# The entrance of the second block: order of the last GLU round, of level six and of the head factors

## What is computed

```
h  = h + conv_glu_ffn(rmsnorm(h))        # gelu(conv3(h Wa)) * (h Wb), then W_down; 11 rounds of 256 columns
z  = rms_norm(x) @ w_in                  # split into lru_x, lru_y, hg_q, hg_f, hg_i, hg_g, cq, ck, cv
ya = rglru_group(...)                    # first branch, a linear recurrence
yb = hgrn2_group(q, f, i, g, ...)        # "third branch" of the change's title: gated linear attention, 4 heads of 64
yb = rms_norm(o per head) * silu(g)
yc = moba_group(cq, ck, cv)              # causal attention, 8 heads of 64
x  = x + concat(rms_norm(ya), yb, rms_norm(yc)) @ w_out
x  = x + relu(rms_norm(x) @ w_ff1)^2 @ w_ff2
```

## Time and profile before

| what | value |
|---|---|
| median of 3 runs | 731.07 us (728.11 to 731.2) |
| profiled execution | 729.23 us, of which 727.5 us are the profile's span |
| PE, share of the span | 97% |
| DVE, ACT, POOL | 74%, 54%, 3% |
| mean granted clock of TensorE | 0.999 |
| chain that ended last | PE 74%, DVE 14%, ACT 8%, issue 3% |

### The profile page before, as it was taken

How to read it: one execution, slowest core, us unless ns; L and a number is a source line. 1 busy time by engine, 2 the same in 40 slices (tenths; PEclk the granted TensorE clock), 3 DMA queues, 4 the chain that set the end, 5 groups by cost and what they waited for, 6 DMA issues and landing times.

```text
span 727.5 us, 14613 instructions
## 1 busy us (share of the span) xinstructions
PE 705.1 (97%) x6156; PEld 665.2 (91%) x6156; DVE 537.0 (74%) x953; ACT 389.5 (54%) x599; POOL 23.9 (3%) x50
## 2 busy tenths in 40 slices
PE   7999999999999999999999999999999999999997
PEld 6998988888999999999999999888899998998995
DVE  6898898556988877777768798965977655666653
ACT  7586458356466354444445683488664334434443
POOL 3001000000000000000000240000000000000000
PEclk9999999999999999999999999999999999999999
DMA  8751253133555555555555534333345555565541
GB/s 246 219 161 59 77 158 116 62 100 134 173 173 176 174 177 194 200 184 174 177 193 197 188 130 163 122 100 125 125 147 183 202 193 175 194 209 175 182 166 58
DMA packets 94701, 115.66 MB, mean 159 GB/s; under 512 B 7972, under 2 KB 83933, under 8 KB 94637
## 3 DMA queue, kind: packets, MB, share of 16 engines
q1 hardware_dynamic: 94244, 114.51, 48.0%
q0 software_dynamic: 128, 0.13, 0.1%
q10 hardware_dynamic: 264, 0.10, 0.1%
HBM read 113.69 MB, written 1.05 MB: 158 GB/s over the span
## 4 chain that ended last, share of the span: by engine, by line
PE 74%; DVE 14%; ACT 8%; issue 3%; POOL 0%; DVEq 0%; POOLq 0%; ACTq 0%
PE psum L1838 16%; PE psum L1839 15%; PE psum L1840 15%; PE psum L2425 4%; PE psum L2423 4%; PE psum L2424 4%; DVE w_lo L1101 4%; ACT w_hi L501 3%; PE psum L2192 2%; PE psum L2190 2%; PE psum L2188 2%; DVE sz L1020 1%; PE psum L1985 1%; PE psum L2020 1%; PE psum L1930 1%
## 5 line engine op out<-in xcount | busy, mean ns | idle before, releaser
L1101 DVE TENSOR_TENSOR w_lo<-w_raw,w_hi 128x2048 fp32r<-128x2048 f32 x105 | 239.4, 2288 | 71.6 <-ACT w_hi L501 71.4
L501 ACT ACTIVATE w_hi<-w_raw 128x2048 fp32r<-128x2048 f32 x105 | 199.1, 1906 | 54.8 <-PE psum L2425 39.4
L1838 PE MATMUL psum<-x2n_hi,w_hi 128*128 128x256 f32 x400 | 114.2, 286 | 2.3 <-DVE w_lo L1101 1.2
L1839 PE MATMUL psum<-x2n_lo,w_hi 128*128 128x256 f32 x400 | 112.0, 280 | 0.0
L1840 PE MATMUL psum<-x2n_hi,w_lo 128*128 128x256 f32 x400 | 111.9, 280 | 0.0
L1838 PE MATMUL psum<-hs_hi,w_hi 128*128 128x256 f32 (+1 forms) x352 | 99.5, 283 | 0.0
L1839 PE MATMUL psum<-hs_lo,w_hi 128*128 128x256 f32 (+1 forms) x352 | 99.1, 282 | 0.0
L1840 PE MATMUL psum<-hs_hi,w_lo 128*128 128x256 f32 (+1 forms) x352 | 99.0, 281 | 0.0
L1838 PEld LDWEIGHTS psum<-x2n_hi,w_hi 128*128 128x128 f32 x400 | 75.2, 188 | 5.6 <-DVE x2n_lo L1558 1.7
L1840 PEld LDWEIGHTS psum<-x2n_hi,w_lo 128*128 128x128 f32 x400 | 76.2, 190 | 0.0
L1839 PEld LDWEIGHTS psum<-x2n_lo,w_hi 128*128 128x128 f32 x400 | 75.1, 188 | 0.6
(11 more groups left out here) (460 smaller groups left out, 1533.6 us busy)
## 6 DMA issues: line engine op xcount, KB each, us to landing
w_raw<-in_w_ff_dram SPq DMA_DIRECT2D x32, 1024.0 KB, 5.3
w_raw<-in_w_in_dram SPq DMA_DIRECT2D x27, 1024.0 KB, 5.3
w_raw<-in_w_up_dram SPq DMA_DIRECT2D x22, 1024.0 KB, 5.1
w_raw<-in_w_down_dram SPq DMA_DIRECT2D x11, 1024.0 KB, 5.0
w_raw<-in_w_o_dram SPq DMA_DIRECT2D x4, 1024.0 KB, 5.2
w_raw<-in_w_out_dram SPq DMA_DIRECT2D x4, 1024.0 KB, 5.2
w_raw<-in_w_ssm_out_dram SPq DMA_DIRECT2D x2, 1024.0 KB, 5.0
w_raw<-in_w_att_out_dram SPq DMA_DIRECT2D x2, 1024.0 KB, 4.9
```

The source lines that it names most:

```text
L501: A.activation(w_hi[:, u % NW, :], raw[:, u % NRAW, :], ACT.Copy).then_inc(sem("hi_ready"), 1)
L1101: V.tensor_tensor(w_lo[:, u % NRAW, :], raw[:, u % NRAW, :], w_hi[:, u % NW, :].bitcast(F32), ALU.subtract).then_inc(sem("lo_ready"), 1)
L1838: T.matmul(out_, lh, rh, start=start, stop=False)
L1839: T.matmul(out_, lh, rl, start=False, stop=False)
```

## The change

Five edits, all of order or of the form of a small product. In the last GLU round both engines' `split_to` for down 10 comes after the gate product: on ACT after the gelu and the copy of up_b, on DVE after `ff_lo` (in `lo_upto`). ACT's high half of hg_q comes right after that of hg_f, ahead of `x2n_hi` and the squares. DVE's low half of cq 0 comes ahead of eight tiny instructions of 2 columns (L1670 to L1677). For the second pair of heads DVE has the low half of cv 0 ahead of `m_max(1)`, and `level(5)` ahead of `m_norm(1)`; PE has `h_scores(6)` ahead of `m_turn(1)`. The head factors are made with tokens on the partitions: 128 x 8 in place of 4 x 256. In the loop of the second norm, ACT's high half of ff1 1 comes after the last two tiles.

```diff
@@ -292,7 +292,6 @@
         sq2 = sb("sq2", [P, 2, 256], F32, k(103552))
         sq3 = sb("sq3", [P, 2, 256], F32, k(107648))
         rst2 = sb("rst2", [P, 256], F32, k(105600))
-        rsm2 = sb("rsm2", [4, 256], F32, k(106624))
         sqs = sb("sqs", [P, 8, 256], F32, k(89216))
         rst1 = sb("rst1", [P, 258], F32, k(112768))
         lru_w = sb("lru_w", [P, 2, 2, P], F32, k(109696))
@@ -789,11 +788,14 @@
                     copy_up_b(i)
                 else:
                     gelu_a(i)
-                split_to(unit_at[(second, i)]["n"] + 3)
+                if i < KF // 2 - 1:
+                    split_to(unit_at[(second, i)]["n"] + 3)
                 if second == "up_b":
                     copy_up_b(i)
                 else:
                     gelu_a(i)
+                if i == KF // 2 - 1:
+                    split_to(unit_at[(second, i)]["n"] + 3)
                 if i == KF // 2 - 2:
                     act.wait_ge(sem("tiny_v"), 1)
                     A.activation(sm("sp_e", 2), sm("sp_ab", 2), ACT.Exp, scale=-1.0).then_inc(sem("tiny_a"), 1)
@@ -805,10 +807,7 @@
                     if i >= 2:
                         need(act, "acc_unit_done", i - 1)
                     A.activation(ff_hi[:, i % 2, m, :], ff[:, i % 2, m, :], ACT.Copy).then_inc(sem("ff_hi"), 1)
-            split_to(unit_at[("down", KF // 2 - 1)]["n"] + 1)
-
-
-            split_to(unit_at[("hg_f", 0)]["n"] + 1)
+            split_to(unit_at[("hg_q", 0)]["n"] + 1)
 
             def x2_square(m):
                 A.activation(sqs[:, m, :], x2[:, m, :], ACT.Square).then_inc(sem("x2_stat_sq"), 1)
@@ -821,7 +820,6 @@
                     x2_square(m // 2)
             for m in range(4, 8):
                 x2_square(m)
-            split_to(unit_at[("hg_q", 0)]["n"] + 1)
             act.wait_ge(sem("x2_stat"), 1)
             A.activation(rst1[:, :], banks[3][:, 0:258], ACT.Sqrt, bias=eps_col, scale=1.0 / D).then_inc(
                 sem("x2_rms"), 1)
@@ -944,7 +942,7 @@
                 scaled("lru_y", m, lru_g, ACT.Gelu_apprx_tanh)
 
             act.wait_ge(sem("hg_stat"), 2)
-            A.activation(rsm2[:, :], banks[5][0:4, 0:256], ACT.Sqrt, bias=eps_col[0:4, :], scale=1.0 / 64).then_inc(
+            A.activation(sm("hg_root", 8), banks[5][:, 0:8], ACT.Sqrt, bias=eps_col, scale=1.0 / 64).then_inc(
                 sem("hg_rms"), 1)
             act.wait_ge(sem("yc_stat"), 4)
             A.activation(rst3[:, :], banks[6][:, 0:256], ACT.Sqrt, bias=eps_col, scale=1.0 / 512).then_inc(
@@ -976,7 +974,7 @@
                     sem("x3_hi"), 1)
                 need(act, "x3_stat_sum", min(m - 1, max(m - 2, 1)))
                 A.activation(sq2[:, m % 2, :], x2[:, m, :], ACT.Square).then_inc(sem("x3_stat_sq"), 1)
-                if m % 2 and m < 6:
+                if m % 2 and m < 4:
                     split_to(unit_at[("w_out2", m // 2)]["n"] + 4)
             split_to(unit_at[("ff1", 0)]["n"] + 2)
             act.wait_ge(sem("norm_sum"), 2)
@@ -1666,6 +1665,7 @@
 
             for m in range(2):
                 scale("hg_f", 0, m, hgf[:, m, :])
+            two_after("hg_f")
             dve.wait_ge(sem("tiny_a"), 3)
             seq(V.tensor_scalar(sm("sp_m", 2), lam, -1.0, 0.0, ALU.mult, ALU.max))
             seq(tt(sm("sp_m", 2), sm("sp_m", 2), sm("sp_l", 2), ALU.add))
@@ -1675,7 +1675,6 @@
             seq(V.tensor_scalar(sm("lb_m", 2), sm("lb_0", 2), TINY, None, ALU.max))
             seq(V.tensor_scalar(sm("lb_c", 2), sm("lb_0", 2), -1.0, 1.0, ALU.mult, ALU.add))
             V.tensor_scalar(sm("n8sp", 2), sm("sp_m", 2), -8.0, None, ALU.mult).then_inc(sem("tiny_v"), 1)
-            two_after("hg_f")
             dve.wait_ge(sem("w2_act"), 4)
             for m in range(2):
                 seq(V.tensor_scalar(hgf[:, m, :], hgf[:, m, :], sm("lb_c", 2)[:, m:m + 1], sm("lb_m", 2)[:, m:m + 1],
@@ -1706,11 +1705,11 @@
             scale("cq", 1, 0, cq[:, 2, :], 0.125)
             level(4)
             scale("cq", 1, 1, cq[:, 3, :], 0.125)
+            two_after("cq", 1)
             m_max(1)
-            two_after("cq", 1)
             scale("ck", 1, 0, ck[:, 2, :])
+            level(5)
             m_norm(1)
-            level(5)
             two_after("ck", 1)
             scale("ck", 1, 1, ck[:, 3, :])
             level(6)
@@ -1743,7 +1742,7 @@
                 dve.wait_ge(sem("w2_act"), 7 + m)
                 tt(xc[:, m, :], lru_r[:, m, :], lru_g[:, m, :], ALU.mult).then_inc(sem("lru_h"), 1)
             dve.wait_ge(sem("hg_rms"), 1)
-            V.reciprocal(rsm2[:, :], rsm2[:, :]).then_inc(sem("hg_r"), 1)
+            V.reciprocal(sm("hg_root", 8), sm("hg_root", 8)).then_inc(sem("hg_r"), 1)
             dve.wait_ge(sem("yc_rms"), 1)
             seq(V.reciprocal(rst3[:, :], rst3[:, :]))
             scale("hg_g", 0, 0, hgg[:, 0, :])
@@ -2264,16 +2263,23 @@
                 last.then_inc(sem("hg_o"), 1)
 
             def hg_stat():
-                for m in range(2):
-                    pe.wait_ge(sem("hgo"), m + 2)
-                    T.matmul(banks[5][0:4, 0:256], sel[:, m, 0, 0:4], hqf[:, m, :], start=(m == 0),
-                             stop=(m == 1)).then_inc(sem("hg_stat"), 1)
+                for t in range(2):
+                    for m in range(2):
+                        pe.wait_ge(sem("hgo"), m + 2)
+                        last = T.matmul(banks[5][:, 4 * t:4 * t + 4], hqf[:, m, P * t:P * t + P], sel[:, m, 0, 0:4],
+                                        start=(m == 0), stop=(m == 1))
+                    last.then_inc(sem("hg_stat"), 1)
 
             def hg_bc():
                 pe.wait_ge(sem("hg_r"), 1)
                 for m in range(2):
-                    T.matmul(banks[4 + m][:, 0:256], selT[0:4, m, :], rsm2[:, :], start=True,
-                             stop=True).then_inc(sem("hg_bc"), 1)
+                    for t in range(2):
+                        for par in range(2):
+                            c = 4 * t + 2 * m + par
+                            last = T.matmul(banks[4 + m][64 * par:64 * par + 64, P * t:P * t + P],
+                                            sm("hg_root", 8)[:, c:c + 1].to_broadcast([P, 64]), ident[:], start=True,
+                                            stop=True, skip_group_check=True)
+                    last.then_inc(sem("hg_bc"), 1)
 
             def m_scores(pr):
 
@@ -2342,8 +2348,8 @@
             unit("cq", 1, x2n, 8, between=both((m_turn, 0), (h_scores, 4)))
             m_scores(1)
             unit("ck", 1, x2n, 8, between=lambda: h_scores(5))
+            h_scores(6)
             m_turn(1)
-            h_scores(6)
 
             def gates_and_level():
                 lru_gates()
```

## The result

The changed kernel took 726.65 us (median of 20 runs), the one before 730.67 us in 20 runs beside them: a ratio of 0.9945, with a 95% interval of 0.9932 to 0.9959. That is 4.0 us less, between 3.0 and 5.0. The time lies in the forecast's range, 1.25 us under the 727.9 us that it named. One of the 20 runs before took 977.54 us, which hardly moves a median.

A forecast was written before the change was run, and what follows sets the result against it. PE, busy 97% of the span, was taken to bound the kernel, with about 7 us of stops as ceiling. Gains 1.8 + 0.35 + 0.43 + 0.65 = 3.2 us off 731.07 gave 727.9 us, range 725.6 to 730.0.

The forecast's parts named there:

- part 1: Last GLU round, first norm and cq 0: h_scores(1) starts at 436.8, a gain of 1.8 us.
- The moved low half collides with POOL: Rival at cq 0: DVE pays 0.8 us beside POOL's masks, part 1 gives 1.0, total 728.7 us; chance 0.1.
- hg_q's high half: ACT's half, moved up, fits between `ff_hi` and the first x2, 407.8 to 409.7; no gain of its own.
- The rival on the slower side: ACT's hg_q half waits for its raw unit; landing after 408.4 delays the norm, up to 736.6 us; chance 0.04.
- named as a sign of being wrong: Signs listed beforehand included ACT waiting for a transfer before hg_q's half, and a PE stop ahead of ff1 1.
- Part 2: Level six, second pair of heads: cv 0 starts at 470.0 instead of 470.36, 0.35 us, bounds 0 and 0.6.
- Part 3: Head factors: shorter reciprocal on DVE, hg_g's evacuation moves from 511.38 to 510.95, a gain of 0.43 us.
- `hg_bc`: Head factors' product on PE, 4 records to 16: extra cost between nothing and 0.8 us, taken as nothing.
- Part 4: Second norm: PE's whole 0.53 us stop at ff1 0 goes, 0.65 us with its restart; bound 0.3 to 0.7.
- barely covered: ff1 1's half, next late after the second norm: DVE ends it at 545.7, PE wants it at 545.8.
- the 0.63 given to one side of it: Chance 0.63 that the measured change lies within 0.5% of the time before.
- the 0.33 given to the other: Chance 0.33 that the changed kernel is faster by over 0.5%.

The follow-up runs named there:

- e10: Changed kernel with POOL's memset of hA moved ahead of the six masks, second profile: 723.74 us, ratio to before 0.9952; end 332.88 us after up_a 10.
- e3: Changed kernel with DVE's eight tiny instructions ahead of the low half of cq 0 again: end 333.29 us after up_a 10, against 333.47.
- e7: Changed kernel with POOL's memset of hA moved ahead of the six masks, first profile: end 333.05 us after up_a 10, against 333.47.
- e5: Changed kernel with ACT's high half of ff1 1 ahead of the second norm's last two tiles again: end 334.28 us after up_a 10, against 333.47.
- e6: Changed kernel with the head factors as 4 rows of 256 tokens again: end 334.22 us after up_a 10, against 333.47.
- e1: Changed kernel with the last GLU round in its old order on ACT and DVE: end 335.10 us after up_a 10, against 333.47.
- e4: Changed kernel with level six of the second pair in its old order on DVE and PE: end 334.03 us after up_a 10, against 333.47.
- e11: e10's kernel with down 10's high half ahead of ACT's last gelu and its low half ahead of DVE's `ff_lo`: 722.06 us, ratio to before 0.9930.
- e8: Changed kernel profiled once more, nothing altered; the changed kernel's three profiles end 333.41 to 333.50 us after up_a 10.
- e9: Changed kernel timed and profiled again, nothing altered: 724.21 us, ratio to before 0.9958.

## Why the prediction was right, and where a term was off

The time was right, and the sum within a tenth: 3.2 us forecast, 3.5 measured. In part this is luck: part 1 gave less than forecast and the other three more. By parts:

| part | forecast | before to after | undone, own stretch | undone, at the end |
|---|---|---|---|---|
| 1, last round, norm, cq 0 | 1.8 | 1.56 | 1.48 | 1.40 |
| 2, level six | 0.35 | 0.51 | 0.49 | 0.56 |
| 3, head factors | 0.43 | 0.46 | 0.55 | 0.75 |
| 4, second norm | 0.65 | 0.86 with w_out2's | 0.70 | 0.81 |

- **Part 1, down to hg_q: right.** On the clock of the profile before (0.61 us less, since up_a 10 begins that much later after) the half of down 10 ran from 402.4 (forecast 402.5), `ff_hi` from 404.2 (404.3), down 10 began at 407.7 (407.9), `x2_pair(0)` at 409.8 (409.9), hg_q's subtraction at 418.5 (418.8). The last is 1.67 us earlier than before, where I had 1.4.
- **Part 1, from hg_q on: the failed step.** "The moved low half collides with POOL" was a rival at 0.1, with DVE paying 0.8; the sum took nothing. The collision came, but not with the low half: both subtractions took 2.28 and 2.29 us, as in the earlier trace rows, and POOL's selects gave way (2.57 and 2.31 us; the same two take 0.44 in e10 and 0.29 in e3, where they miss the subtractions). It was the memset and a product of `hgf`, 0.97 for 0.41. The earlier trace rows held the sign of it: a tiny instruction beside the same memset took 0.98. I read that as a price already paid, since the subtraction behind it began 0.07 us later all the same. Moved one instruction on, it met one for whose end the next has to wait. Hence 1.56 and not 1.8 or more, and the stop at 430.31; with the memset out of the way h_scores(1) lies 1.95 (e7) and 2.15 us (e10) ahead of before.
- **cq 0's stop went, and was worth nothing.** I wrote that the tiny instructions stay on DVE's path and that DVE is 1.4 us early only; e3 shows it. PE started cq 0 early and waited for `hgq` instead.
- **hg_q's high half: right at nothing.** ACT waited 1.11 us for PE (down 9) before it, not for a transfer, and was done at 410.36, before `x2n_hi` at 410.84. The rival on the slower side needed a late transfer and had none. It was near: in e5, e6, e7 and e10 this wait of ACT, 0.77 to 1.00 us, ended with the transfer, which the prediction had named as a sign of being wrong. The half still began at 16.93 to 17.16 in the count from up_a 10 (17.32 here), so it delayed nothing.
- **Part 2: size off, 0.35 against 0.5.** h_scores(6) gained 1.13 us on h_scores(5)'s start, as forecast. From it to cv 0 it took 1.72 where I had 1.9.
- **Part 3: 0.46 between hg_stat and w_out2 1, 0.43 forecast.** The reciprocal of 128x8 took the 0.20 taken for it, hg_g's first group is late next (0.64 from PE). For `hg_bc` I took nothing between nothing and 0.8: from its start to hg_g's next matmul it took 1.02 us. The Trainium skill's rule ("TensorE: Matmul & The Clock Gate", "The mechanism"), that a weight load overlaps running matmuls only with other row groups, would have made it longer (the same section excepts loads into a background weight buffer). Sixteen such pairs in 1.02 us, 0.064 each, are no slower than the 64-column tiles of the earlier trace rows, and no slower than the four products before, which took 1.06 in the same count.
- **Part 4: 0.65 forecast, 0.70 undone.** The stop shrank from 0.53 to 0.21 only, because PE came to ff1 0 0.6 us earlier after w_out2 1 than it had before (16.44 against 17.06 us), as its matmuls came faster (below). Without the edit this gain would have gone into the longer stop that e5 shows; and in e3, where PE was as slow as before, the stop is gone, as forecast. ff1 1's half, "barely covered", was not quite: DVE ends it at 543.70 and ff1 1 begins at 543.76, 0.25 us after the matmul before it, where the beat is 0.12. So PE waited some 0.13 us for it, too little for a bracket; this too was named as a sign of being wrong.

Whether the gain is over 0.5% no step of the kernel decides: 3.5 us are 0.48% of the time, right at the bound, between the 0.63 given to one side of it and the 0.33 given to the other.

## What to carry to other kernels

Where an engine stands idle for another's weight half, ask where both could do it in idle time they have: in the last round reordering gave 1.6 us, and using both engines' gaps 0.6 more. A stop that goes is worth only what the next late thing leaves; cq 0's was worth nothing, as its successor was already late on the same engine. An instruction that collides with nothing where it stands can do so when its neighbours move by a microsecond, so look at the other engines' timelines at the new times.

## What the runs showed of the hardware

**PE has two beats.** The same matmuls of 256 columns, at a granted clock of 1.00, come every 0.1133 or every 0.1177 us, and keep to it through long stretches. Two profiles of the changed kernel over the same 20 us of the first block (window: length, PE busy and records, clock, DMA share, GB/s), the first at 391.11 for up_a 10 and the second at 387.59:

```profile
300.00:320.00 20.00, 20.00 (x171) 1.00 0.54 177
```

```profile
300.00:320.00 20.00, 20.00 (x175) 1.00 0.63 211
```

From the first matmul of down 0 to that of up_a 10 the first took 141.94 us (249.17 to 391.11), the second 138.99 (248.60 to 387.59); so counted the thirteen profiles of this study fall in two groups: before, the first one after and e1 to e4 at 141.9 to 142.2 us, e5 to e11 at 139.0. Here lie 3 of the 3.6 us between the spans of these two runs, 724.6 and 721.0, and it is why whole times of single runs decide nothing: the beat alone is worth nearly what the change is. The beat changes at restarts of PE, and in no stretch without an interruption. The expectation of e8 had this right but put its worth at up to 1 us, where one stretch alone makes 3; its rival, that the beat hangs on the instructions, fails, as one kernel shows the same stretch at both beats. In w_out2 1 to 3 the beat was slow before and fast after, which made 0.6 of the 3.26 us gained at ff1 0:

```profile
529.90 0.28 PE L1839 MATMUL psum<-ycat_hi,w_lo 128*128 128x256 f32 x1
530.02 0.28 PE L1837 MATMUL psum<-ycat_hi,w_hi 128*128 128x256 f32 x1
530.13 0.28 PE L1838 MATMUL psum<-ycat_lo,w_hi 128*128 128x256 f32 x1
```

It was slow there in e3 too (17.07 us from w_out2 1 to ff1 0, against 16.44), and e3 lost nothing by it at the end: PE was at ff1 0 0.45 us later and at the transposes 0.09 earlier. What sets the beat stays open. e1 to e4 ran on one chip, e5 to e8 on a second, e9 to e11 on a third, and no chip shows both groups, so the chip may have a part in it; nothing was tried on that. The 12 runs of the changed kernel on the third chip lie between 721.03 and 728.43 us, as far apart as the 20 of the first series, though its profiles there all have the fast beat. That speaks against the chip alone, but the single runs behind those times have no trace to show their beat.

**POOL and DVE hold each other up, and not in every pairing.** A select on POOL beside DVE's subtraction of two tensors: POOL pays (0.44 to 2.57, 0.29 to 2.31), DVE nothing. A memset beside the same subtraction (e3): neither pays. The memset beside DVE's products with one tensor: DVE pays, ending 0.15 us after the memset. Who pays was each time the one that began later, or at the same moment (DVE's tiny instruction at 426.50 before), so order may decide it and not the kind of instruction. The Trainium skill, "SBUF — State Buffer", section "SBUF: two separate sides", describes a port pair that the two engines hold for a whole instruction: DVE when it reads two SBUF tensors, and then only against a POOL instruction that reads, or when it runs in a two-port mode. It also says that the one that starts first gets the pair. The three cases agree with it, if the products with one tensor run in such a mode, which no run here shows.
